# Where the fourth weight unit of an embeddings' product is split, at the end of two mixers of a block kernel

## The reference, cut to what matters

```python
out = mixer(rms_norm(h, pre_norm[i]))            # 256 x 2048, last step a product with w_out
h = h + rms_norm(out, post_norm[i])
gate = jax.nn.sigmoid(rms_norm(h, ple_norm[i]) @ ple_w_gate[i])
h = h + (p[i] @ ple_w_proj[i]) * gate            # p: 256 x 256, the embeddings
```

## Time and profile before

| | |
|---|---|
| median of three runs | 2434.01 us (2433.85 to 2434.53) |
| the profiled execution | 2434.6 us, of which its span is 2432.7 us |
| busy: TensorE matmul, weight load | 2422.3 us, 2082.3 us |
| busy: VectorE, ScalarE, GpSimd | 1717.1 us, 1381.2 us, 82.9 us |
| granted TensorE clock, mean | 0.999 |

### The profile page before, as it was taken

How to read it: one execution, slowest core, us unless ns; L and a number is a source line. 1 busy time by engine, 2 the same in 40 slices (tenths; PEclk the granted TensorE clock), 3 DMA queues, 4 the chain that set the end, 5 groups by cost and what they waited for, 6 DMA issues and landing times.

```text
span 2432.7 us, 34024 instructions
## 1 busy us (share of the span) xinstructions
PE 2422.3 (100%) x12667; PEld 2082.3 (86%) x12667; DVE 1717.1 (71%) x2080; ACT 1381.2 (57%) x1830; POOL 82.9 (3%) x100
## 2 busy tenths in 40 slices
PE   9999999999999999999999999999999999999998
PEld 8888888888889999878888888888988888888887
DVE  7675757788765656786656767665666666679997
ACT  6444444556656666565755556565645545556655
POOL 0000000001100000010000000000000000000001
PEclk9999999999999999999999999999999999999999
DMA  8666666676556554575585564454566666657785
GB/s 314 197 188 187 189 184 187 194 242 215 183 178 182 173 164 141 211 229 195 163 234 169 155 178 144 165 181 154 175 186 180 188 191 180 189 172 212 239 234 162
DMA packets 237363, 462.46 MB, mean 190 GB/s; under 512 B 15265, under 2 KB 60753, under 8 KB 236220
## 3 DMA queue, kind: packets, MB, share of 16 engines
q1 hardware_dynamic: 230960, 435.94, 57.6%
q0 software_dynamic: 5888, 24.34, 3.9%
q10 hardware_dynamic: 396, 0.59, 0.2%
HBM read 448.68 MB, written 2.69 MB: 186 GB/s over the span
## 4 chain that ended last, share of the span: by engine, by line
PE 99%; DVE 1%; ACT 0%; issue 0%; ACTq 0%; DVEq 0%
PE ps L835 25%; PE ps L837 13%; PE ps L801 12%; PE ps L803 12%; PE ps L802 12%; PE ps L985 6%; PE ps L986 6%; PE ps L987 6%; PE ps L759 1%; PE ps L866 1%; PE ps L867 1%; PE ps L868 1%; PE ps L1473 1%; PE ps L1244 0%; PE ps L1232 0%; PE ps L1431 0%
## 5 line engine op out<-in xcount | busy, mean ns | idle before, releaser
L2468 DVE TENSOR_TENSOR w_lo<-raw,w_hi 128x1024 fp32r<-128x1024 f32 x689 | 842.1, 1228 | 466.7 <-ACT w_hi L1643 446.5
L1643 ACT ACTIVATE w_hi<-raw 128x1024 fp32r<-128x1024 f32 x689 | 726.9, 1060 | 651.7 <-PE ps L837 358.8
L835 PE MATMUL ps<-x_hi_lo,w_hi 128*128 128x512 f32 x2336 | 821.5, 394 | 0.0
L837 PE MATMUL ps<-x_hi_lo,w_lo 128*128 128x256 f32 x2336 | 661.0, 283 | 0.0
L835 PEld LDWEIGHTS ps<-x_hi_lo,w_hi 128*128 128x128 f32 x2336 | 439.1, 188 | 101.3
L801 PE MATMUL ps<-w_hi,x_hi_lo 128*128 128x512 f32 (+3 forms) x1184 | 461.9, 390 | 0.0
L803 PE MATMUL ps<-w_hi,x_hi_lo 128*128 128x512 f32 (+3 forms) x1184 | 453.7, 383 | 0.0
L802 PE MATMUL ps<-w_lo,x_hi_lo 128*128 128x512 f32 (+3 forms) x1184 | 452.7, 382 | 0.0
L837 PEld LDWEIGHTS ps<-x_hi_lo,w_lo 128*128 128x128 f32 x2336 | 439.5, 188 | 0.0
L1820 ACT ACTIVATE w_hi<-raw 128x1024 fp32r<-128x1024 f32 x207 | 215.6, 1052 | 159.7 <-PE ps L987 136.7
L2476 DVE TENSOR_TENSOR w_lo<-raw,w_hi 128x1024 fp32r<-128x1024 f32 x207 | 248.9, 1222 | 34.7 <-ACT w_hi L1820 34.5
(11 more groups left out here) (469 smaller groups left out, 2732.6 us busy)
## 6 DMA issues: line engine op xcount, KB each, us to landing
raw<-in_w_up SPq DMA_DIRECT2D x160, 512.0 KB, 4.2
raw<-in_pool_w_in SPq DMA_DIRECT2D x126, 512.0 KB, 3.9
raw<-in_w_in SPq DMA_DIRECT2D x96, 480.0 KB, 4.0
raw<-in_w_down SPq DMA_DIRECT2D x84, 512.0 KB, 5.5
raw<-in_pool_w_out SPq DMA_DIRECT2D x64, 512.0 KB, 5.0
raw<-in_ple_w_gate SPq DMA_DIRECT2D x64, 512.0 KB, 4.3
raw<-in_mla_w_in SPq DMA_DIRECT2D x56, 448.0 KB, 3.6
raw<-in_pool_w_group SPq DMA_DIRECT2D x32, 512.0 KB, 4.1
```

The costliest lines, as they stand in the source:

```text
L835: pe.matmul(bank, w_hi[:, slot, cols], xs[:, k].rearrange("p s n -> p (s n)"), start=k == 0, stop=False, skip_group_check=True)
L837: last = pe.matmul(bank[:, 0:T], w_lo[:, slot, cols], xs[:, k, 0, :], start=False, stop=k == nkt - 1, skip_group_check=True)
L1643: act.activation(w_hi[:, t.slot(), :], raw[:, slot, :], ACT.Copy).then_inc(S("w_hi"), 1)
L2468: dve.tensor_tensor(w_lo[:, t.slot(), :], raw[:, u % RAW, :], w_hi[:, t.slot(), :].bitcast(F32), ALU.subtract)\
```

## The change

At the end of both mixers the fourth unit of the embeddings' product is copied by ScalarE ahead of the last chunk's squares instead of behind the first read-out, and subtracted by VectorE ahead of the mean instead of between the first two updates. The wait in `layer_end`'s first chunk is counted with one unit fewer ahead of it, so that it means the same product as before: the unit count is now one further when it is reached.

```diff
@@ ScalarE, layer_end, L1903
                     s = t.n["chunk"] % 2
                     t.add("chunk")
-                    act.wait_ge(S("w_used"), t.product(RING - LEAD + 1))
+                    act.wait_ge(S("w_used"), t.product(RING - LEAD))
                 read_out(s, lambda tt: proj[:, tt, c * 512:(c + 1) * 512])
-                if c == 0:
-                    hi(1)
                 if c == 2:
@@ ScalarE, end of layer 0, L1957
         act.activation(rc_cos, red, ACT.Sin).then_inc(S("rope_tables"), 1)
-        hi(1)
+        hi(2)
         t.add("chunk", 4)
         square_mixed(3)
@@ ScalarE, end of layer 1, L2125
         hi(3)
         t.add("chunk", 2)
-        for c in (2, 3):
-            square_mixed(c, "mla_out", 6)
+        square_mixed(2, "mla_out", 6)
+        hi(1)
+        square_mixed(3, "mla_out", 6)
@@ VectorE, layer_end, L2833
                 evacuated(dve, mixer)
                 dve.wait_ge(S("squared_out"), NCH + 3)
+            lo(1)
             mean(slot, D)
             inverse(slot)
@@ VectorE, layer_end, L2848
             update(0)
-            skip(1)
+            t.add("chunk")
             update(1)
             for c in range(2):
                 skip(1)
```

## The result

The changed kernel takes 2438.06 us (median of 22 runs, 2436.47 to 2439.67), the kernel before 2434.05 (22 runs beside them, 2433.34 to 2434.92). The ratio is 1.0017 (95% interval 1.0011 to 1.0022), 4.0 us. That is under the 0.2% set for a difference, so it counts as the same, and it lies within the range. But it is 4.0 us slower where 2.1 were forecast, and a ratio of 1 lies outside the interval. In two kernels of the experiments one execution was far longer than all others (2619.66 us in run 2, 6712.2 us in run 10); it is left out of the ratios, and without it the medians given would be 0.05 and 0.02 us lower.

What follows compares the result with a forecast made beforehand. TensorE's matmul stream was taken to bound the kernel. The subtraction costs 1.03 us in layer 0 and 1.09 in layer 1, all else 0: 2.1 us on the median 2434.01, so 2436.1 us, range 2434.3 to 2438.9.

Steps and rivals of the forecast that it cites:

- The bound and the sign: TensorE's matmul stream bounds the kernel; at both mixers' ends its waits hold 1.0 us, and (c) costs nothing below 0.
- (a): ScalarE's fourth-unit copy, 1.06 us, moved ahead of the last squares, is hidden in both layers: cost 0.
- (b): Without that copy between ScalarE's first two read-outs the second comes 1.06 us sooner, but nobody waited: worth 0.
- (d): VectorE's updates and gate subtractions, the freed raw slot and GpSimd's second product shift behind the mean: all 0.
- Point (c), layer 0: VectorE's subtraction ahead of the mean, taking its turn before GpSimd's product, makes the mean end 1.03 us later.
- Point (c), layer 1: The same subtraction, VectorE again taken first, costs 1.09 us; GpSimd first would cost 2.3. VectorE first at both: chance 0.45.
- one turn lost: Rival: GpSimd's product comes before VectorE's subtraction in one layer, 1.1 + 2.3 = 3.4 us, 2437.4 us, chance 0.27.
- The clock: Rival: GpSimd first in layer 1, TensorE's clock falls after 2.6 us idle, costing 2.9 us; about 2440.8 us, chance 0.06.
- both turns lost: Rival: GpSimd's product comes before VectorE's subtraction in both layers, 4.6 us, 2438.6 us, chance 0.10 with the clock kept.

Runs made afterwards that it cites:

- run 2: The whole change, but VectorE's subtraction of the fourth unit stands ahead of its wait for the squares: 2433.54 us against 2433.77 for the kernel before.
- run 10: The changed kernel measured once more beside the kernel before: 2437.56 us against 2433.89, ratio 1.0016.
- run 1: Only ScalarE's copy moved ahead of the squares, VectorE's subtraction left as in the kernel before: 2433.84 us against 2433.77, ratio 1.0000.
- run 3: The whole change in layer 0 alone: 2434.79 us against 2433.77 for the kernel before, ratio 1.0003.
- run 8: The kernel before with two filler copies on ScalarE between root and first read-out of layer 1: 2436.64 us, +2.88, ratio 1.0009.
- run 4: The whole change in layer 1 alone: 2437.89 us, +4.12 against the kernel before, ratio 1.0016.
- run 9: The kernel before with four filler copies on ScalarE between root and first read-out of layer 1: 2438.03 us, +4.27, ratio 1.0018.
- run 5: The changed kernel with GpSimd's last gain product waiting for the mean in both layers: 2434.49 us against 2433.76 for the kernel before, ratio 1.0003.
- run 6: The change in layer 1 alone, with GpSimd's last product waiting for the fourth unit's subtraction: 2434.04 us against 2433.74 for the kernel before, ratio 1.0002.
- run 7: The kernel before with one filler copy on ScalarE between root and first read-out of layer 1: 2434.08 us, +0.34.

## Why the prediction was right, and where it was wrong

**The bound and the sign** were right. TensorE's stream is the kernel, L801 is where it waits, and the chain squares, mean, root, read-out has no slack. Nobody waited for the fourth unit, so there was nothing to win against the push of the mean.

**Points (a), (b) and (d)** were right: run 1 shows the first two, and TensorE waits at no new line in the gate product.

**Point (c), layer 0** was right to the hundredth: 1.03 us forecast, 1.03 in the timelines of three executions, +1.02 in the times of run 3.

**Point (c), layer 1** is the step that failed: "I take VectorE first at both places". There the sum had stood level with GpSimd in the rows of before, and the subtraction comes 0.05 to 0.06 us behind it. The text named what might cost the lead, the second semaphore that the subtraction has to pass. Whether it does stays open: in layer 1 the subtraction starts 0.06 us later than the sum did (after 1.76 us of idleness, not 1.70), but in layer 0, where it passes the same semaphore, it starts no later (1.59 us in both kernels). Its own price for that case was right: 2.3 us worked out, 2.21 measured. So the case that came true is the rival "one turn lost", 3.4 us on paper and 1.03 + 2.21 = 3.24 us in the timelines. That GpSimd's lead made the difference between 1.1 and 2.2 us is read from these timelines; no run turned the order round within one layer.

**The clock.** That it may fall in layer 1 once the turn is lost was a rival at 0.06, and it happens in most executions. Both of its numbers were off. The point from which it decides was read from the tail as 2.6 us of idleness; run 8 shows the fall at a gap of 1.81 us. And the price, 2.9 us from half of the 5.7 us at the start of the kernel, wasn't borne out: the granted clock of that stretch is 1.00 in the profile, so its rows can't price a fall. The price is 1.4 to 1.55 us in the four traces that show a fall: 4.29 us (run 4) and 4.45 us (the changed kernel, runs 8 and 9) to the transposes in place of 2.90. The clock stayed at the lower level for some 3.4 us, where 5.7 were assumed. With the true price the rival would have been 3.24 + 1.5 = 4.7 us, about 2438.8, which stays under 0.2%. The 22 executions lie around the two cases: 2434.05 + 3.24 = 2437.3 without the fall and 2438.8 with it, and the median of 2438.06 between them. So it was partly luck that the median lies in the range: its upper end, 2438.9, was put there for both turns lost, which didn't happen, and the fall, which did, had been priced to lie outside.

The Trainium skill ("TensorE: Matmul & The Clock Gate", Part 1) has the array go back to 1.2 GHz when idle and earn 2.4 by work. The runs agree with both halves: in the changed kernel the granted clock is 0.50 behind the gap of 2.83 us and 1.00 again from about 1094. They add that the same gap of 2.8 us can keep the level in one execution and lose it in another.

**Left open.** What decides between a fall and none at the same gap wasn't found; two executions of the changed kernel were traced and one of each other. By the mean clock of the executions, none of 11 is at 0.998 in each of runs 5, 6, 3 and 7 (gaps of 0.87, 0.87, 1.07 and 1.14 us), 6 of 11 at 1.81 (run 8), 9 of 11 at 2.78 (run 4), 6 of 11 at 3.13 (run 9), and 14 of 22 and 4 of 11 for the changed kernel at 2.8. So falls were seen from 1.81 us on and none up to 1.14; between the two nothing was tried. Above 1.81 these counts show no order, but the rounding of the clock to three places blurs them: three executions of run 9 have 0.999 and took 2438.03, 2438.86 and 2438.95 us, as long as those with 0.998. Such shares would also explain why runs 3 and 4 add up to 5.1 us and not to 4.0, since a median moves with the share; that is argued, not shown.

## What to carry to other kernels

Before moving work "behind a wait and ahead of" something, look at who stands in the chain that the bottleneck engine waits for. Here the same subtraction cost 0 ahead of the wait and up to 2.2 us behind it, because it met the other engine that the same semaphore released.

Here the two engines released by one semaphore start within 0.06 us of each other, and where they exclude each other that lead is worth a whole product. A wait that puts the less urgent one behind is one line, and in run 5 it took the cost from 4.0 us to 0.7.

If a change opens a gap in TensorE's stream, add the clock to the sum as a case of its own: here nothing in 44 executions with gaps up to 1.14 us, and +1.5 us in a part of the executions with gaps of 1.81 us and more, where it also widens the spread.

## What the runs showed of the hardware that was not expected

- The clock can fall after TensorE has resumed: in the changed kernel it was at 1.00 for 0.85 us behind a gap of 2.83 us, and then at 0.50; in run 9 it was at 1.00 for 0.60 us behind a gap of 3.13. In run 8 it fell within 0.2 us of the first matmul (behind 1.81 us), and in run 4 it fell inside the gap of 2.78 us.
- At gaps of 2.83 and 2.82 us of the same kernel it fell in the first traced execution and not in the second.
- A GpSimd product that waits on a semaphore starts 0.16 us behind the instruction that releases it, long enough for a second, short VectorE instruction to go first (run 6). One that was only blocked took the very next turn, ahead of L2598, in both layers of the changed kernel.
- A table load of 1.28 us stands in ScalarE's queue between squares and root. Once GpSimd holds the mean for less long, this load is what the root waits for (run 2, layer 1: the mean ends at 1084.90, the load at 1085.48, and the root starts at 1085.50), so it has to be moved before any gain ahead of it counts.
